# Identity multiplications at the boundaries between stages, taken out of a four-layer kernel on one core

## The chip, the core and the metric

The kernel runs on one NeuronCore of a Trainium2 chip. The metric is the time of one execution on the device, in microseconds (us). A core has a matrix engine (TensorE, PE in the rows; its weight loads are PEld), VectorE (DVE), ScalarE (ACT), GpSimd (POOL) and SyncE (SP), which here issues the weights' DMAs. TensorE's clock has two levels, 1.2 and 2.4 GHz; the profile gives the granted clock as a share of the full one, 0.50 or 1.00, or a mean between them.

## The reference

Two blocks of two layers each work on 256 rows of 1024 features, float32:

```python
for i in range(2):                                   # layers 0 and 1
    q, k, v = project_qkv(x, w_qkv[i], cos, sin)
    a = moba_attention(q, k, v) if i == 0 else sliding_window_attention(q, k, v, sinks)
    x = layer_norm(alpha * x + a @ w_o[i], ln_mix_g[i], ln_mix_b[i])
    f = swiglu(x, ...) if i == 0 else moe_swiglu(x, w_router, ...)   # 8 experts, top 2
    x = layer_norm(alpha * x + f, ln_ffn_g[i], ln_ffn_b[i])
    x = x + (p[i] @ w_ple_proj[i]) * sigmoid(x @ w_ple_gate[i])
for l in range(2):                                   # layers 2 and 3
    h = hybrid_mixer(rmsnorm(x, pre_mix_norm[l]), ...)   # delta rule and dilated attention
    x = x + rmsnorm(h, post_mix_norm[l])
    h = conv_glu_ffn(rmsnorm(x, pre_ffn_norm[l]), ...)
    x = x + rmsnorm(h, post_ffn_norm[l])
```

None of it contains the multiplications that this case is about.

## The kernel before

One core holds X, the 256 rows, as two row tiles of 128 rows (t = 0, 1). Every large product is made of three matmuls: an operand is split into a high and a low part (w_hi and w_lo for weights, xT_hi and xT_lo or aT_hi and aT_lo for activations), and mm3 (line 770) issues high x high, high x low and low x high. Weights stream in as units of 128 x 2048 values through six raw buffers; ScalarE casts the high part (line 520), VectorE subtracts the low part (line 525).

Each engine runs one program written out by hand, in order, with semaphore waits between engines. For this case TensorE's order at a boundary between two stages matters. A stage that starts from X needs X transposed. At a boundary X is being normalised, row tile after row tile, by VectorE and ScalarE. TensorE then does, in this order:

- turn_tile for t = 0: it waits until X of that tile is ready, and transposes it by 8 matmuls (line 750) in layers 0 and 1, or multiplies it by a diagonal matrix of the row scales, by 16 records of fp32 matmuls (line 748), in layers 2 and 3;
- keep_warm(n, b): it waits until bank b is free, and issues n matmuls of an identity by 512 columns of constants into that bank; nobody reads them, and the next turn writes over them;
- turn_tile for t = 1;
- tile_ready: it waits until the turned tiles are copied out and split (ScalarE's cast of xT_hi, line 1345; VectorE's xT_lo, lines 1793 and 1796, in layers 2 and 3 after line 1955, which applies the norm's weights);
- the next stage: the dense feed-forward in layer 0 (features, by mm3), the router and the experts in layer 1, the delta-rule mixer on entry into layers 2 and 3, and the feed-forward of layers 2 and 3.

```python
            def keep_warm(n, b):

                if M.free[b].n:
                    pe.wait_ge(M.free[b].sem, M.free[b].n)
                for _ in range(n):
                    nc.tensor.matmul(bank[b][:, :], ident, cst[:, 0:512], start=True, stop=True)
```

It is called with WARM_START once before the first stage (line 1282), with WARM_LN between attention and feed-forward of layers 0 and 1 (line 1286), and through enter (lines 1313 to 1323) with WARM_RMS on entry into layer 3 and before the feed-forward of layers 2 and 3; on entry into layer 2 the count is 0. The three constants stand in line 40.

Of the kernel before, what the change touches and what calls it, by code (L numbers as in the profile page):

```python
# [36 lines left out]
FF2 = 2816  # L37
NE = 8
UNIT = 2048
WARM_START, WARM_LN, WARM_RMS = 6, 5, 4  # L40
RAW = 6
SPLIT = 3
NEG = -1.0e30
# [2541 lines left out]
```

How the kernel before makes its waits and increments, by code:

```python
        def wait_loaded(E, eng, i):  # L485
            slot, n = i % RAW, 16 * (i // RAW + 1)
            if E.ev.turn is not None:
                n = n + E.ev.turn * (16 * TURN // RAW)
            eng.wait_ge(E.loaded[slot].sem, n)
            return raw[:, slot, :]
# [5 lines left out]
        def unit(E, pe, key, base=None):  # L496
            i = index(key, base)
            pe.wait_ge(*E.lo.at("unit", key_of(i)))
            return w_hi[:, place(i), :], w_lo[:, place(i), :]
# [11 lines left out]
        def split_hi(E, ac, i):  # L512
            src = wait_loaded(E, ac, i)
            back = i - SPLIT - (1 if any(i - SPLIT <= w < i for w in whole) else 0)
            if E is V and i < SPLIT:
                ac.wait_ge(E.groups.sem, 1 + E.ev.turn * plan.per.get("ovf_groups", 0))
            elif back >= 0:
                ac.wait_ge(*reader(E, back))
            nc.scalar.copy(w_hi[:, place(i), :], src).then_inc(*E.hi.mark("unit", i))
# [1 line left out]
        def split_lo(E, ve, i):  # L522
            ve.wait_ge(*E.hi.at("unit", i))
            nc.vector.tensor_tensor(w_lo[:, place(i), :], raw[:, i % RAW, :], w_hi[:, place(i), :].bitcast(F32), ALU.subtract) \
                .then_inc(*E.lo.mark("unit", i))
# [26 lines left out]
            def overflow_loads():  # L553
                sp.wait_ge(*flag_done.at())
                r = sp.value_load(flag_i[0:1, 0:1], min_val=0, max_val=1)
                with sp.If(r > 0):
                    sp.wait_ge(*M.put.at("last"))
# [83 lines left out]
            def load_both():  # L641
                gp.wait_ge(*params.last())
                for L in (2, 3):
```

## Time and profile before

| | |
|---|---|
| time before, median of 3 executions | 2372.84 us (2371.3 to 2373.51) |
| the profiled execution | 2372.58 us, of which 2370.8 us is the span from the first to the last instruction |
| TensorE busy in the span | 2233.2 us (94%) |
| VectorE, ScalarE, GpSimd busy | 1717.1, 1371.4, 54.3 us |
| mean granted TensorE clock | 0.969 |
| DMA | 573.37 MB, mean 242 GB/s |

How to read it: an engine's busy time is the time in which one of its instructions runs; matmuls overlap one another, so that the busy time of TensorE is the union of them. A matmul at half clock counts as just as busy as one at full clock, but takes longer: a busy share says nothing of speed, and the granted clock has to be read beside it. Where TensorE idles, the timeline names what it waited for.

### The profile page before, as it was taken

To read this page: it belongs to the slowest core of one execution; us is meant where nothing else is said; L and a number is where in the kernel's file an instruction comes from. 1 tells how busy PE (TensorE), PEld (TensorE's weight loads), DVE (VectorE), ACT (ScalarE), POOL (GpSimd) and SP (SyncE) were. 2 spreads that over 40 slices of the span, in tenths; PEclk is the share of its full clock that TensorE was granted. 3 is DMA by queue.
4 is the path that set the end of the run, shared out by engine and by line. 5 is a ranking of instruction groups with operands and counts; after the bars stand their busy time and mean duration, and the time that the engine had idled before them with its cause. 6 is when DMAs were issued, how large, how long until landed. Compare 5 with 4: busy or idle time off the path is not lost. (4 is left out here: it accounts for less than half of the span.)

```text
span 2370.8 us, 32516 instructions
## 1 busy us (share of the span) xinstructions
PE 2233.2 (94%) x12412; PEld 1907.0 (80%) x12412; DVE 1717.1 (72%) x1876; ACT 1371.4 (58%) x1423; POOL 54.3 (2%) x72
## 2 busy tenths in 40 slices
PE   7899999789999999999999999799899989889998
PEld 5689997568888888888888878598779978877997
DVE  5554546658888888888888898676657667665766
ACT  5433334537777777777777777462554446254444
POOL 2000000010000000000000020000000000000000
PEclk9799999989999999999999999899899999989999
DMA  9355554339999999999999999532325543132550
GB/s 391 141 200 180 193 180 176 108 107 378 378 378 372 384 373 378 377 381 373 377 376 380 372 385 371 190 125 72 125 107 179 195 160 110 72 116 103 182 195 37
DMA packets 81800, 573.37 MB, mean 242 GB/s; under 512 B 9552, under 2 KB 9664, under 8 KB 15984
## 3 DMA queue, kind: packets, MB, share of 16 engines
q1 hardware_dynamic: 76320, 545.82, 60.8%
q0 software_dynamic: 5376, 26.12, 3.0%
q8 instruction: 71, 1.16, 0.2%
q14 instruction: 33, 0.27, 0.0%
HBM read 564.03 MB, written 17.83 MB: 245 GB/s over the span
## 5 line engine op out<-in xcount | busy, mean ns | idle before, releaser
L525 DVE TENSOR_TENSOR w_lo<-raw,w_hi 128x2048 fp32r<-128x2048 f32 x508 | 1163.3, 2300 | 352.1 <-ACT w_hi L520 350.2
L520 ACT CAST w_hi<-raw 128x2048 fp32r<-128x2048 f32 x508 | 969.2, 1911 | 519.2 <-PE bank L770 513.9
L770 PE MATMUL bank<-w_hi,xT_hi 128*128 128x512 f32 x1184 | 468.2, 395 | 10.7 <-DVE w_lo L525 5.9
L770 PE MATMUL bank<-w_hi,xT_lo 128*128 128x512 f32 x1184 | 461.4, 390 | 0.0
L770 PE MATMUL bank<-w_lo,xT_hi 128*128 128x512 f32 x1184 | 460.9, 389 | 0.0
L770 PE MATMUL bank<-xT_hi,w_hi 128*128 128x256 f32 x1344 | 383.6, 285 | 6.9 <-DVE xT_lo L1796 5.0
L770 PE MATMUL bank<-xT_hi,w_lo 128*128 128x256 f32 x1344 | 383.0, 285 | 0.0
L770 PE MATMUL bank<-xT_lo,w_hi 128*128 128x256 f32 x1344 | 382.9, 285 | 0.0
L770 PE MATMUL bank<-w_hi,aT_hi 128*128 128x512 f32 x864 | 346.4, 401 | 15.3 <-DVE aT_lo L2007 9.5
L770 PE MATMUL bank<-w_hi,aT_lo 128*128 128x512 f32 x864 | 338.8, 392 | 0.0
L770 PE MATMUL bank<-w_lo,aT_hi 128*128 128x512 f32 x864 | 338.8, 392 | 0.0
L770 PEld LDWEIGHTS bank<-w_hi,xT_hi 128*128 128x128 f32 x1184 | 222.3, 188 | 63.9 <-DVE w_lo L525 11.6
L770 PEld LDWEIGHTS bank<-xT_hi,w_hi 128*128 128x128 f32 x1344 | 260.8, 194 | 8.8 <-DVE xT_lo L1796 5.3
L770 PEld LDWEIGHTS bank<-xT_lo,w_hi 128*128 128x128 f32 x1344 | 260.6, 194 | 1.2
L770 PEld LDWEIGHTS bank<-xT_hi,w_lo 128*128 128x128 f32 x1344 | 260.4, 194 | 0.0
L770 PEld LDWEIGHTS bank<-w_hi,xT_lo 128*128 128x128 f32 x1184 | 222.2, 188 | 47.1
L770 PEld LDWEIGHTS bank<-w_lo,xT_hi 128*128 128x128 f32 x1184 | 222.4, 188 | 45.0 <-issue 0.7
L770 PEld LDWEIGHTS bank<-w_hi,aT_hi 128*128 128x128 f32 x864 | 164.2, 190 | 50.3 <-issue 18.4
L770 PEld LDWEIGHTS bank<-w_hi,aT_lo 128*128 128x128 f32 x864 | 163.5, 189 | 35.5
L770 PEld LDWEIGHTS bank<-w_lo,aT_hi 128*128 128x128 f32 x864 | 164.2, 190 | 30.9
L1479 ACT ACTIVATE arena<-bank,fcw 128x256 f32<-128x256 f32 x88 | 44.9, 560 | 61.3 <-PE bank L770 61.3
L1615 ACT COPY arena<-bank 128x512 f32<-128x512 f32 x24 | 14.1, 586 | 91.9 <-PE bank L1164 91.9
(318 smaller groups left out, 1700.8 us busy)
## 6 DMA issues: line engine op xcount, KB each, us to landing
raw<-in_wu_eg SPq DMA_DIRECT2D x112, 1024.0 KB, 7.2
raw<-in_wu_eu SPq DMA_DIRECT2D x112, 1024.0 KB, 7.2
raw<-in_wu_ed SPq DMA_DIRECT2D x112, 1024.0 KB, 7.1
raw<-in_wu_up SPq DMA_DIRECT2D x44, 1024.0 KB, 4.8
raw<-in_wu_ffn_gu SPq DMA_DIRECT2D x28, 1024.0 KB, 4.8
raw<-in_wu_in SPq DMA_DIRECT2D x28, 1024.0 KB, 4.8
raw<-in_wu_down SPq DMA_DIRECT2D x22, 1024.0 KB, 4.8
raw<-in_wu_ffn_d SPq DMA_DIRECT2D x14, 1024.0 KB, 4.8
```

Source lines behind the costliest of these rows:

```text
L520: nc.scalar.copy(w_hi[:, place(i), :], src).then_inc(*E.hi.mark("unit", i))
L525: nc.vector.tensor_tensor(w_lo[:, place(i), :], raw[:, i % RAW, :], w_hi[:, place(i), :].bitcast(F32), ALU.subtract) \
L770: mm = nc.tensor.matmul(o, l[i], r[j], start=(first and n == 0), stop=(last and n == 2), skip_group_check=not lone)
L1479: ins = nc.scalar.activation(buf[:, s % 2, m, :], bank[b + half][:, m * S:(m + 1) * S], ACT.Identity, bias=fcw[:, c, 3:4], scale=fcw[:, c, ...
L1615: nc.scalar.copy(dn["Xl"][:, t * DN_H:(t + 1) * DN_H, :], bank[t][:, :].rearrange("p (h n) -> p h n", n=P)) \
```

## The change

Two constants are set to zero. The loops in keep_warm then issue nothing at the boundaries; the wait before them and all else stays, and the six multiplications at the start stay too.

```diff
-WARM_START, WARM_LN, WARM_RMS = 6, 5, 4
+WARM_START, WARM_LN, WARM_RMS = 6, 0, 0
```

## Rows read from the trace of the kernel before

**Rows 1.** The page, TensorE's granted clock in 40 equal slices, in tenths.

```profile
PEclk9799999989999999999999999899899999989999
```

**Rows 2.** Windows of two feed-forward stages: length, busy PE PEld DVE ACT POOL, clock, DMA.

```profile
127.50:356.00 228.50, 228.50 (x1634) 216.95 (x1635) 115.72 (x80) 83.96 (x54) 0.00 (x0) 0.99 0.53 187
...
2176.00:2349.00 173.00, 173.00 (x1248) 164.28 (x1247) 121.18 (x144) 84.58 (x84) 0.00 (x0) 1.00 0.44 155
```

**Rows 3.** The line of the identity multiplications: ns min/median/max, first and last start.

```profile
L765 PE MATMUL bank<-cst x56: 592/592/1220, 9.6 to 2164.5; 128*128 128x512 f32 x56
...
  issue: 12.2, 44
```

**Rows 4.** Timeline, layer 0, attention to feed-forward: start us, us, instruction, [idle before <-releaser].

```profile
118.02 1.03 PE L750 MATMUL bank<-cst,X 128*128 128x128 f32 x8
...
118.89 4.46 PE L765 MATMUL bank<-cst 128*128 128x512 f32 x10
...
123.09 1.28 DVE L1921 SCALAR_TENSOR_TENSOR X<-R,small,vec 128x1024 f32<-128x1024 f32 x1
...
124.43 1.09 PE L750 MATMUL bank<-cst,X 128*128 128x128 f32 x8 [1.08 <-DVE X L1921]
...
127.42 0.35 PE L770 MATMUL bank<-xT_hi,w_hi 128*128 128x256 f32 x1 [1.90 <-DVE xT_lo L1793]
```

**Rows 5.** Timeline, layer 1, attention to router.

```profile
507.96 1.28 DVE L1921 SCALAR_TENSOR_TENSOR X<-R,small,vec 128x1024 f32<-128x1024 f32 x1
...
509.31 0.14 PEld L750 LDWEIGHTS bank<-cst,X 128*128 128x128 f32 x1 [0.25 <-DVE X L1921]
...
509.72 1.04 PE L750 MATMUL bank<-cst,X 128*128 128x128 f32 x8
```

**Rows 6.** Timeline, layer 2, mixer to feed-forward; layer 3 repeats it from 2161.49 on.

```profile
1745.96 3.60 PE L765 MATMUL bank<-cst 128*128 128x512 f32 x8
...
1750.87 2.05 PE L748 MATMUL bank<-R,X 128*128 128x128 f32 x16 [1.31 <-DVE R L1946]
...
1752.13 1.52 DVE L1955 TENSOR_TENSOR arena<-bank,prew 128x512 f32<-128x512 f32 x2
...
1755.41 0.35 PE L770 MATMUL bank<-xT_hi,w_hi 128*128 128x256 f32 x1 [2.50 <-DVE xT_lo L1796]
```

**Rows 7.** Timeline, entry into layer 3.

```profile
1957.65 2.05 PE L748 MATMUL bank<-R,X 128*128 128x128 f32 x16
...
1959.49 1.29 DVE L1796 TENSOR_TENSOR xT_lo<-arena,xT_hi 128x512 fp32r<-128x512 f32 x2 [1.89 <-ACT xT_hi L1345]
...
1963.80 0.28 PE L1096 MATMUL bank<-xT_hi,wba_hi_lo 128*16 128x256 f32 x1 [4.09 <-DVE xT_lo L1796]
```

**Rows 8.** Windows behind the five boundaries, and one at full clock (131.23).

```profile
127.82:131.23 3.41, 3.41 (x18) 3.41 (x17) 3.41 (x2) 0.00 (x0) 0.00 (x0) 0.50 0.59 177
131.23:134.64 3.41, 3.41 (x31) 3.41 (x30) 0.27 (x1) 0.00 (x0) 0.00 (x0) 1.00 1.01 423
513.53:516.94 3.41, 3.41 (x18) 2.06 (x16) 3.41 (x2) 1.64 (x1) 0.00 (x0) 0.50 0.44 119
520.35:527.18 6.83, 5.53 (x26) 5.43 (x27) 4.79 (x27) 2.63 (x4) 1.64 (x2) 0.50 0.35 143
1755.98:1759.39 3.41, 3.41 (x19) 3.41 (x18) 3.41 (x2) 0.12 (x1) 0.00 (x0) 0.50 0.29 65
...
1964.19:1967.60 3.41, 3.41 (x19) 2.49 (x17) 1.45 (x1) 0.36 (x1) 0.00 (x0) 0.50 0.28 46
2172.40:2175.82 3.42, 3.42 (x19) 3.42 (x18) 2.63 (x2) 0.00 (x0) 0.00 (x0) 0.50 0.50 170
```

**Rows 9.** Turns with no multiplications before them: timeline rows, and the window around the second.

```profile
1505.46 1.97 PE L750 MATMUL bank<-cst,X 128*128 128x128 f32 x8 [4.87 <-DVE X L1921]
...
1539.13 6.31 PE L748 MATMUL bank<-R,X 128*128 128x128 f32 x32 [4.09 <-DVE R L1946]
...
1537.52:1544.35 6.83, 5.22 (x24) 5.22 (x25) 2.88 (x7) 5.57 (x10) 0.00 (x0) 0.50 0.00 0
```

## The prediction

> **What bounds the kernel now.** I read the page first, for the share of TensorE and for its clock; then the windows of the long dense stages, to learn whether time lost by TensorE comes back anywhere; then the line of the removed instructions; then the timeline around each place where they stand; and last the windows at either clock level, to price the clock. The page's clock row shows a kernel that is mostly at full clock, 9 tenths, with dips to 8 and 7 [rows 1]: the clock falls somewhere in many slices. The windows of the feed-forward stages of layers 0 and 3 have TensorE busy for the whole of 228.5 us and 173.0 us [rows 2]. There is no idle time in them in which a late start could be made good. So whatever TensorE loses at the door of such a stage reaches the end of the program in full, and whatever it does while it would otherwise stand idle costs nothing.
>
> The multiplications in question are the second kind of thing on their face. They are the 28 fp32 matmuls of line 765, each of which the trace holds as two records, 56 in all [rows 3]; nobody waits for them. 6 stand at the start and stay; 5 stand at each of two boundaries and 4 at each of three, 22 in all, and go. In layer 0 the ten records of five matmuls run for 4.46 us from 118.89, and end at 123.35. The turn of the second row tile (8 transposes, line 750) needs X, which VectorE writes from 123.09 to 124.37, and starts at 124.43 [rows 4]. TensorE has 1.08 us to spare after its last idle multiplication: these do not delay the turn.
>
> **The change part by part.**
>
> Removed instructions on TensorE's queue. In four of the five places nothing is won. Layer 0: 1.08 us to spare, as said [rows 4]. Boundary to the feed-forward of layer 2: the turn starts at 1750.87, right when the diagonal of line 1946 is there [rows 6], and the four matmuls, which take 3.60 us, were issued 4.9 us earlier; that of layer 3 repeats it. Entry of layer 3: the turn's first matmul starts at 1957.65 [rows 7], 0.05 us after the last filler has streamed; I take 0. Boundary of layer 1 is the exception: X is ready at 507.96 + 1.28 = 509.24, the turn's first weights load at 509.31, and yet its matmuls come at 509.72 [rows 5], because the fifth filler is still streaming. Here the removal wins about 0.35 us. The wait for the bank that stands before the fillers stays in the program, and is one that the turn has to pass anyway: 0.
>
> The clock, term A, the turns. What the fillers change is what TensorE did before the clock is granted. Layer 0 without them: TensorE is dense until about 119.05 (1.03 us from 118.02), then idle until 124.43, 5.4 us instead of 1.1, then busy for 1.09 us, then idle until 127.42 [rows 4]. The trace has two boundaries of just this shape and without fillers. Entering layer 2, after 4.09 us of idling, the 32 records of both turns took 6.31 us, 0.197 us each, in a stretch at 0.50 [rows 9]; 16 of them at full clock take 2.05 us, 0.128 each [rows 6]. And the turn at 1505.46, after 4.87 us of idling, took 1.97 us for 8 transposes [rows 9] against 1.09 [rows 4]. So I expect the second turn of a boundary at 1.2 GHz. It lies on the path: at layer 0 the chain goes turn, cast on ScalarE, subtraction on VectorE, first multiplication. Layer 0: 1.97 - 1.09 = +0.9 us. Layer 1: only 3.8 us pass between the first turn and the second, so the clock may fall in the middle of it: between 0 and +0.9, I take +0.5. Layers 2 and 3, feed-forward: 16 x 0.197 = 3.15 against 2.05, +1.1 us each, all of it on the path, as VectorE takes the turned halves one after the other at 1752.13 [rows 6]. Entry of layer 3: VectorE is not done with the first tile before 1959.49 + 1.29 = 1960.78 [rows 7], when a turn at half clock that began at 1957.65 is through at 1960.8: 0, at most 0.2. A = 0.9 + 0.5 + 1.1 + 0 + 1.1 = 3.6 us (bounds 0 and 4.2).
>
> Term B, the dense stage behind the turn. Today, too, every one of the five boundaries has a fall: just after the stage has begun there is one stretch of 3.4 us at 0.50 with 18 or 19 matmuls in it, where the next 3.4 us at 1.00 hold 31 [rows 8]. The fillers do not prevent the fall in this execution; they put it off until the stage runs. One such stretch costs 12 of 31 matmuls, 12 x 0.11 = 1.4 us. Without fillers the clock is low already when the stage begins, and has to be earned back by dense work: the half-clock part of the stage may be somewhat shorter than 3.4 us, or up to nearly 6.8, the length of the two low stretches that had idle time at their head [rows 8, 9]. The extra is so between 0 and +1.4 us for each; I take the middle, 0.7, for layers 0, 2 and 3 (feed-forward). In layer 1 the stage behind is the router's 24 short matmuls, half of which run low already: +0.35. Entry of layer 3: a full idle gap of 4.09 us stands between the turn and the stage whatever the fillers do [rows 7]: 0. B = 3 x 0.7 + 0.35 = 2.45 us (bounds 0 and 5).
>
> Term C, executions other than the profiled one. That all five falls happen is a matter of how the idle gap of 1.9 to 2.5 us lies to the moments at which the clock is set. Other executions may be spared some that the longer gap never is. The profiled execution took 2372.58 us and the median of the three others is 2372.84, so it was not an unlucky one by much. I take 0.8 of a fall, 0.8 x 1.4 = 1.1 us, with bounds 0 and 3 falls, 4.2 us.
>
> Sum: -0.35 + 3.6 + 2.45 + 1.1 = +6.8 us on the profiled execution's 2372.58 (of which 2370.8 is the span), 2379.4; the median stands 0.26 above it, so 2379.6 us, 0.29% slower.
>
> A rule against term A: the transposes of line 750 took 1.97 us in a stretch at 0.50 [rows 9] and 1.09 at 1.00 [rows 4], so here they follow the granted clock. The Trainium skill, "TensorE: Matmul & The Clock Gate", Part 4: PE-mode transpose, says that full clock doesn't engage for transposes, which do not count as busy work in the same way. By it the turns of layers 0 and 1 would lose nothing, 1.4 us less in the sum; the trace disagrees on their speed, and no row separates whether they count as work.
>
> **The rivals.**
>
> 1. Slower by the clock, as summed. For it: the falls after 4 and 5 us of idling [rows 9], and TensorE without a gap behind [rows 2].
>
> 2. Only a shift. The clock falls earlier and so is back earlier: each boundary keeps one low stretch, part of it under idle time. Then B is 0 or negative, C is 0, and half of A stays hidden by the work of ScalarE and VectorE: 1.8 - 0.35 = +1.5 us, 2374.3 us, no measurable change. For it: every boundary has its fall today [rows 8]. Against it: the low stretches with idle time at their head are twice as long.
>
> 3. Not slower: the fillers' place in TensorE's queue. They hold the turn of layer 1 back by 0.35 us [rows 5], and the one of layer 3's entry by at most 0.1 [rows 7]. If the clock took no notice of them (a multiplication by an identity might not count as work), only this is left: 2372.84 - 0.45 = 2372.4 us. It decides if the second turns still run at 1.00 after the change. Against it: layer 2's entry without fillers ran its turns at 0.50, layer 3's with them at 1.00 [rows 7, 9].
>
> 4. Worse: the low clock feeds itself, since a slower turn makes the gap longer for the next. The whole 6.8 us at half clock at four boundaries, instead of 3.4: 4 x 1.4 = 5.6, with A's 4.2 and C's 4.2, +14, 2386.8 us.
>
> 5. Fewer than named. The change speaks of six boundaries; the diff sets two constants, and the sixth, the entry of layer 2, has a count of 0 already. That costs nothing in the sum, which counts 22 instructions.
>
> **How the numbers follow.** Rival 1: 0.70. Rival 2: 0.14. Rival 3: 0.06. Rival 4: 0.10. The likeliest gives 2379.6 us. About 4.7 us (0.2%) is what a measurement of this kernel can tell from no change. The likeliest case itself runs from +2.5 to +13 (A, B and C near their bounds), so part of it, about 0.10, falls within 0.2%. The range reaches down to 2374.0, into the shift, and up to 2387.5, over most of case 4. Slower by over 0.2%: 0.60 + 0.10 + a little of case 2, hence 0.72. Within 0.2%: 0.25. Faster: 0.03, since the rows allow a gain of no more than half a microsecond, and only something that they do not show could give more.
>
> **What would show it.** In the profile of the changed kernel: line 765 with 12 records, all at the start. The second turn of layer 0 at about 2.0 us instead of 1.09, and those before the feed-forward of layers 2 and 3 at about 3.1 instead of 2.05, in windows at 0.50 (term A). The low stretch at each of these doors beginning before the turn and reaching 3.4 to 6.8 us into the stage, the same stages still without a gap (term B). Layer 1's turn 0.4 us sooner after X. Entry of layer 3 unchanged in length. The prediction is wrong if the turns keep 1.00; or if the clock is back before the stage begins, which is the shift; or if the stages behind show idle time that takes the loss in.

## Result, and the profile after

| | before | after |
|---|---|---|
| median of 16 executions | 2372.53 us | 2375.79 us |
| ratio to before, with its 95% interval | | 1.0017 (1.0009 to 1.0025) |
| profiled execution's span | 2370.8 us | 2373.6 us |
| mean granted clock | 0.969 | 0.963 |
| TensorE busy | 2233.2 us | 2218.8 us |

The change makes the kernel slower, by 0.17% or 4 us (2 to 6), where +6.8 us was forecast. The ratio is not that of the two medians: these lie 3.3 us apart, the means of the same executions 4.0. (One execution of a kernel further down, the half-filled one, took 4459 us and is left out of its ratio.) TensorE does 44 records fewer, is busy for 14.4 us less, and the program ends later. The page's clock row shows little of it: against [rows 1], slices 8 and 30 (counted from 1) have 8 tenths where they had 9, and slice 2 has 8 where it had 7. Slice 30 holds the door of layer 2's feed-forward; slices 2 and 8 hold none of the edited places.

```profile
PEclk9899999889999999999999999899889999989999
```

Line 765 is left with the 12 records at the start:

```profile
L765 PE MATMUL bank<-cst x12: 592/592/1222, 9.6 to 16.0; 128*128 128x512 f32 x12
```

At the door of layer 0's feed-forward (timeline of after, start us, us, instruction, idle before it; to be read beside [rows 4]):

```profile
120.57 1.28 DVE L1921 SCALAR_TENSOR_TENSOR X<-R,small,vec 128x1024 f32<-128x1024 f32 x1
...
121.95 1.94 PE L750 MATMUL bank<-cst,X 128*128 128x128 f32 x8 [5.41 <-issue]
...
125.63 0.55 PE L770 MATMUL bank<-xT_hi,w_hi 128*128 128x256 f32 x1 [1.74 <-issue]
```

The reader sees the idle gap of 5.41 us, the turn at 1.94 us instead of 1.09, and the stage's first multiplication at 0.55 us instead of 0.35: the turn and the stage's beginning are both at half clock. From X to the stage it is 5.06 us, and was 4.33: +0.73 us. (The trace as a whole stands 2.5 us earlier at this point, ahead of the first edit: the first stage began 1.2 us earlier, and a low stretch in the attention of layer 0 is shorter. That is why places are compared by their own lengths here.)

At the door of layer 1's router, against [rows 5], first the router's first multiplication in before, then after:

```profile
512.75 0.28 PE L770 MATMUL bank<-xT_hi,wr_hi 128*8 128x256 f32 x1 [1.99 <-DVE wr_lo L2377]
```

```profile
509.45 1.29 DVE L1921 SCALAR_TENSOR_TENSOR X<-R,small,vec 128x1024 f32<-128x1024 f32 x1
...
510.84 1.70 PE L750 MATMUL bank<-cst,X 128*128 128x128 f32 x8 [3.77 <-issue]
514.34 0.37 PE L770 MATMUL bank<-xT_hi,wr_hi 128*8 128x256 f32 x1 [1.80 <-DVE wr_lo L2377]
```

The turn comes 1.39 us after X is begun instead of 1.76: 0.37 us won, as no filler is in the way. Its 1.70 us instead of 1.04 take that back: from X's begin to the router it is 4.89 us, and was 4.79.

At the door of layer 2's feed-forward, against [rows 6]; layer 3's repeats it (turn 3.75 us, and 6.25 us from turn to stage):

```profile
1751.89 3.75 PE L748 MATMUL bank<-R,X 128*128 128x128 f32 x16 [4.80 <-issue]
1754.05 0.69 DVE L1955 TENSOR_TENSOR arena<-bank,prew 128x512 f32<-128x512 f32 x1 [0.87 <-PE bank L748]
...
1755.69 0.69 DVE L1955 TENSOR_TENSOR arena<-bank,prew 128x512 f32<-128x512 f32 x1 [0.94 <-PE bank L748]
...
1758.14 0.55 PE L770 MATMUL bank<-xT_hi,w_hi 128*128 128x256 f32 x1 [2.49 <-DVE xT_lo L1796]
```

VectorE now waits for each half of the turn (0.87 and 0.94 us). From turn to stage it is 6.25 us, and was 4.54: +1.71 us.

At the entry of layer 3, against [rows 7]:

```profile
1961.45 3.46 PE L748 MATMUL bank<-R,X 128*128 128x128 f32 x16 [3.45 <-issue]
1963.24 1.29 DVE L1796 TENSOR_TENSOR xT_lo<-arena,xT_hi 128x512 fp32r<-128x512 f32 x2 [1.89 <-PE bank L748]
...
1967.55 0.28 PE L1096 MATMUL bank<-xT_hi,wba_hi_lo 128*16 128x256 f32 x1 [2.63 <-DVE xT_lo L1796]
```

The turn is slow as well, 3.46 us, and it costs nothing: turn to stage 6.10 us, and was 6.15.

How much of each stage runs at half clock. Windows of after, cut at the stage's first multiplication: length, busy PE PEld DVE ACT POOL, clock, DMA (against [rows 8]):

```profile
118.57:125.63 7.06, 1.94 (x9) 1.60 (x9) 6.04 (x10) 3.26 (x4) 1.59 (x3) 0.50 0.70 245
125.63:128.81 3.18, 3.18 (x15) 3.18 (x16) 3.18 (x2) 0.00 (x0) 0.00 (x0) 0.50 0.38 108
1750.15:1758.14 7.99, 3.75 (x16) 3.52 (x17) 5.48 (x11) 4.47 (x8) 0.00 (x0) 0.50 0.00 0
1758.14:1763.80 5.66, 5.66 (x26) 5.66 (x27) 4.09 (x2) 0.70 (x1) 0.00 (x0) 0.50 0.48 178
...
2173.70:2176.80 3.10, 3.10 (x14) 3.10 (x15) 3.10 (x2) 0.69 (x1) 0.00 (x0) 0.50 0.10 21
```

Before, each stage had 3.4 us of it. Now the clock is low for 7 to 8 us ahead of the stage, and then for 3.18, 5.66 and 3.10 us in it. The low subtraction that VectorE makes some 10 us into the stage tells what that costs. Layer 2, the same instruction in before and in after, two fences:

```profile
1764.91 2.29 DVE L525 TENSOR_TENSOR w_lo<-raw,w_hi 128x2048 fp32r<-128x2048 f32 x1 [5.41 <-ACT w_hi L520]
```

```profile
1768.63 2.29 DVE L525 TENSOR_TENSOR w_lo<-raw,w_hi 128x2048 fp32r<-128x2048 f32 x1 [6.40 <-ACT w_hi L520]
```

It is 3.72 us later, and the stage began 2.73 us later: 0.99 us in the stage. In layers 0 and 3 the same step gives -0.08 and -0.11 us.

So the five boundaries of this pair of profiles cost: layer 0 0.73 - 0.08 = 0.65; layer 1 0.1; layer 2 1.71 + 0.99 = 2.7; entry of layer 3 0; layer 3 1.67 - 0.11 = 1.6. Together 5.0 us. The spans differ by 2.8: -2.5 us of that arose ahead of the first edit, so that the program behind it is 5.3 us longer. The rest of the program, which has no edit in it, went otherwise in the two executions, up and down:

```profile
2101.00:2152.50 51.50, 42.69 (x216) 32.67 (x215) 23.09 (x67) 25.81 (x63) 1.05 (x2) 0.83 0.23 82
352.20:500.90 148.70, 127.45 (x648) 97.56 (x647) 94.14 (x219) 69.78 (x144) 1.58 (x3) 0.95 0.35 126
```

```profile
2104.50:2153.50 49.00, 40.45 (x216) 30.98 (x215) 22.99 (x67) 25.81 (x63) 1.05 (x2) 0.86 0.25 86
350.30:502.40 152.10, 131.41 (x648) 100.71 (x647) 94.41 (x219) 69.81 (x144) 1.58 (x3) 0.92 0.34 123
```

The first fence is before, the second after; each row covers the same instructions (216 and 648 matmul records in both). The attention of layer 3 is 2.5 us shorter at a clock of 0.86 instead of 0.83, the stretch from the end of layer 0's feed-forward to layer 1's attention 3.4 us longer at 0.92 instead of 0.95. Against such swings only many executions of each kernel carry a verdict.

### The profile page after: what moved, and what is told of

The parts are those of the page before. It is cut to its first block and busy times, and to the rows that moved or that the text cites. A ratio compares the mean times of both kernels' runs of the same rounds, so it can differ in the third digit from the quotient of the medians.

```text
span 2373.6 us, 32428 instructions
## 1 busy us (share of the span) xinstructions
PE 2218.8 (93%) x12368; PEld 1904.4 (80%) x12368; DVE 1718.2 (72%) x1876; ACT 1372.0 (58%) x1423; POOL 58.0 (2%) x72
```

## Experiments

The fillers are the identity multiplications of keep_warm and whatever stands in their place. The theory: they are worth what they do to TensorE's clock, and nothing else. The rivals: they only hold up TensorE's queue (a gain if they go); or the low stretch is merely shifted. Medians are in us, ratios to the kernel before on the same chip, with 95% intervals.

### Which boundaries

```diff
-WARM_START, WARM_LN, WARM_RMS = 6, 5, 4
+WARM_START, WARM_LN, WARM_RMS = 6, 0, 4
```

> Only the fillers of layers 0 and 1 are taken out (counts 6, 0, 4). Theory (slow clock at the door of the stage): in the pair of profiles the boundary of layer 0 cost +0.65 us and that of layer 1 +0.1 us, and an execution that is spared falls today loses more, so +0.5 to +2.5 us, middle +1. The second turn of layer 0 takes about 1.95 us instead of 1.09. Rival (the fillers only hold up TensorE's queue): -0.35 us, turn at 1.09.

Measured: 2374.57, ratio 1.0009 (1.0001 to 1.0018). Its second turn in layer 0, and the window around it:

```profile
121.58 1.94 PE L750 MATMUL bank<-cst,X 128*128 128x128 f32 x8 [5.42 <-issue]
...
120.30:130.50 10.20, 7.19 (x32) 6.84 (x33) 8.16 (x7) 1.63 (x3) 1.55 (x3) 0.50 0.60 212
```

The clock is at half for 10.2 us, 5.2 of them behind the stage's start at 125.26, where the changed kernel had 3.18: here the stage's part was the large one.

```diff
-WARM_START, WARM_LN, WARM_RMS = 6, 5, 4
+WARM_START, WARM_LN, WARM_RMS = 6, 5, 0
```

> Only the fillers of layers 2 and 3 are taken out (counts 6, 5, 0). Theory: in the pair of profiles +2.75 and +1.6 us at the two feed-forward doors and 0 at the entry of layer 3, so +2.5 to +4.5 us, and together with the run that takes out those of layers 0 and 1 the two make up the whole change's +4. The two turns take about 3.75 us instead of 2.05. Rival (only a shift of the low stretch): +1.5 us or less.

Measured: 2374.30, ratio 1.0015 (1.0006 to 1.0024). The turn of layer 2 took 3.75 us and the stage began 6.34 us after it, against 3.75 and 6.25 us in the changed kernel. Both halves of the change cost time, as expected, the first barely clear of its interval. Their sum, +5.7 us by the ratios (+5.4 by the medians), and the whole change's +4 lie within each other's intervals; the +3.6 of layers 2 and 3 (+2.6 by the medians) is within what was expected of them, and the queue's -0.35 is excluded for layers 0 and 1.

### Filling the gap behind the second turn

```diff
                 turn_tile((L, "mix"), 1, lambda t: x_ready.at(L, "mix", t))
+                keep_warm(2, turn_bank((L, "mix"), 0, 0))
...
                         turn_tile((L, which), t, lambda t: prenorm.at(L, which, t), True)
+                    keep_warm(2 if which == "mix" else 4 if L == 3 else 0, turn_bank((L, which), 0, 0))
```

> All fillers of before stay, and further ones are added behind the second turn of the same five boundaries (2, 2, 2, 2, and 4 at the entry of layer 3), into the bank that the first tile has left, to fill the idle gap of 1.9 to 4.1 us before the stage. Theory: the falls that before has behind each boundary (18 matmuls in 3.4 us instead of 31) vanish; each is worth 1.4 us, so up to -7 us, -4 to -6 in the mean as some executions are spared some already. If the clock doesn't see such multiplications as work, or if the fillers hold up the stage: 0 to +2 us.

Measured: 2364.53, ratio 0.9969 (0.9957 to 0.9981), 7.4 us faster than before. The windows behind the boundaries in its trace:

```profile
125.13:128.54 3.41, 3.40 (x28) 3.41 (x29) 3.41 (x2) 0.00 (x0) 0.00 (x0) 1.00 0.63 198
1752.90:1756.30 3.40, 2.85 (x24) 2.88 (x25) 3.40 (x3) 1.21 (x1) 0.00 (x0) 1.00 0.00 0
1961.10:1964.50 3.40, 3.39 (x29) 3.02 (x30) 1.84 (x1) 0.36 (x1) 0.00 (x0) 1.00 0.17 36
510.60:514.00 3.40, 2.95 (x25) 2.00 (x25) 2.74 (x2) 2.87 (x4) 0.00 (x0) 1.00 0.30 110
2168.90:2172.00 3.10, 3.10 (x28) 3.10 (x27) 0.75 (x1) 0.33 (x1) 0.00 (x0) 1.00 0.90 365
```

All of them are at 1.00, with 28 or 29 matmuls (fewer where the window begins ahead of the stage or the router has ended) where [rows 8] has 18 or 19: the five falls are gone. By the start times of the same matmuls in this trace and in that of before, that makes the heads of the five stages 6.2 us shorter (about 1.5 us each, the router 0.2). What is won at the entry of layer 3 is lost again, as the clock falls once more in its stage, 25 us on, at 1989.4; and 2.5 us of the whole come from the attention of layer 3, which has no edit. This is the theory's strongest test. More work without a reader was added (24 records) and the kernel became faster. It beats both kernels of the case, and the gain is a little more than the 4 to 7 us that were expected.

With the same additions, but the fillers ahead of the second turn taken out:

```diff
-WARM_START, WARM_LN, WARM_RMS = 6, 5, 4
+WARM_START, WARM_LN, WARM_RMS = 6, 0, 0
```

> The fillers before the second turn are out, as in the change, and the ones behind it are in (2, 2, 2, 2, 4). Theory: the 5.4 us gap ahead of the second turn lets the clock fall before the turn (term A stays, 3 to 4 us), but the low stretch is paid off by fillers instead of the stage's own matmuls, so that the stage's part (term B) mostly goes: between 0 and +3 us against before, 1 to 4 us faster than the change. If only the total of fillers mattered, not their place, it would equal before.

Measured: 2369.18, ratio 0.9992 (0.9984 to 1.0001). The door of layer 2:

```profile
1751.44 3.75 PE L748 MATMUL bank<-R,X 128*128 128x128 f32 x16 [4.79 <-issue]
1754.99 2.71 PE L765 MATMUL bank<-cst 128*128 128x512 f32 x4
1757.69 0.36 PE L770 MATMUL bank<-xT_hi,w_hi 128*128 128x256 f32 x1
```

The turn is at half clock, 3.75 us; four filler records take 2.71 us instead of 1.88, being partly at half clock themselves; and the stage begins at full clock, 0.36 us for its first matmul. Term A is there, and the low part of the stage is gone, today's as well as what term B added. By the medians the kernel is 6.6 us faster than the changed one (5.9 by the ratios), which is more than the 1 to 4 us expected, and 4.7 us slower than the one with both gaps filled (5.5 by the ratios); from before it can't be told apart. So filling the gap behind the turn is worth about 6 us where the one ahead is open and about 7 where it is filled (2371.7 to 2364.5), and filling the gap ahead 4 to 5 us, each give or take 2 us.

```diff
                 def enter(which, warm):
+                    if L == 2 and which == "in":
+                        keep_warm(4, turn_bank((L, which), 0, 0))
...
+                    keep_warm(2 if which == "mix" else 4 if L == 3 else 2, turn_bank((L, which), 0, 0))
```

> The kernel with both gaps filled, plus the sixth boundary, the entry of layer 2, that has no fillers in before: 4 ahead of its first turn and 2 behind its second. Theory: the 32 records of the turns there fall from 6.31 us to about 4 and the low stretch behind them goes: 1.5 to 4 us faster than the kernel with both gaps filled, 2360 to 2363 us. If the fall there comes from the embedding gate's own tail and not from the gap: no change, 2364.5.

This is the kernel with both gaps filled, and the entry of layer 2 besides. Measured: 2364.11, ratio 0.9964 (0.9953 to 0.9976). The turns of the sixth boundary, in the kernel with both gaps filled and in this one (two fences):

```profile
1537.31 6.20 PE L748 MATMUL bank<-R,X 128*128 128x128 f32 x32 [4.09 <-DVE R L1948]
...
1546.37 0.37 PE L1096 MATMUL bank<-xT_hi,wba_hi_lo 128*16 128x256 f32 x1 [2.86 <-DVE wba_hi_lo L2462]
```

```profile
1536.15 3.84 PE L748 MATMUL bank<-R,X 128*128 128x128 f32 x32 [0.65 <-DVE R L1950]
...
1543.95 0.28 PE L1096 MATMUL bank<-xT_hi,wba_hi_lo 128*16 128x256 f32 x1 [2.25 <-DVE wba_hi_lo L2464]
```

The turns fell to 3.84 us as expected, but the stage begins only 1.3 us sooner after them (7.80 us for 9.06), as 2.25 us of idle time are left behind the fillers, and the clock still falls in it. In the medians 0.4 us is to be seen, less than the intervals can tell; the expected gain of 1.5 us and more did not come.

### How much filling, and of what kind

```diff
-WARM_START, WARM_LN, WARM_RMS = 6, 5, 4
+WARM_START, WARM_LN, WARM_RMS = 6, 3, 2
```

> Counts 6, 3, 2 instead of 6, 5, 4: the fillers cover half of the first gap, 2.6 of 5.4 us in layers 0 and 1 and 1.7 of 4.9 in layers 2 and 3. If the clock needs only some work in the gap: equal to before, 2371.5. If any long idle stretch makes it fall: layers 2 and 3 cost most of what taking all out does, layer 0 and 1 little: +1 to +3.5 us.

Measured: 2375.84, ratio 1.0017 (1.0008 to 1.0026): half of the filling is worth no more than none in the whole time, give or take 2 us. Its profile says something else of the boundaries. The second turns of layer 1 (1.09 us), of layer 2 and of layer 3's entry (2.05 us each) kept full clock, and those of layer 0 (1.96 us) and of layer 3's feed-forward did not. From a door's turn to its stage it is 0.7 us longer than before in layer 0 and 1.7 in layer 3, and unchanged in the other three, where the changed kernel lost 2.2 us more. What made the profiled execution as long as the changed kernel's is a place without an edit: the stretch between layer 0's feed-forward and layer 1's attention, 3.4 us longer than before here as there. The rows are layer 2's turn, then layer 3's fillers, which end at 2166.99, and turn. The gap of 3.04 us is the same, and only in layer 3 is the turn at half clock:

```profile
1754.50 2.05 PE L748 MATMUL bank<-R,X 128*128 128x128 f32 x16 [3.04 <-DVE R L1946]
...
2165.11 1.88 PE L765 MATMUL bank<-cst 128*128 128x512 f32 x4
2170.03 3.78 PE L748 MATMUL bank<-R,X 128*128 128x128 f32 x16 [3.04 <-DVE R L1946]
```

Transposes in the place of the multiplications:

```diff
-                    nc.tensor.matmul(bank[b][:, :], ident, cst[:, 0:512], start=True, stop=True)
+                    for c in range(8):
+                        nc.tensor.transpose(bank[b][:, (c % 4) * P:(c % 4 + 1) * P], cst[:, (c % 4) * P:(c % 4 + 1) * P], ident)
```

> Each filler of before becomes 8 transposes of 128 by 128 constants, about as long (8 x 0.109 = 0.87 us against 0.86). If transposes count as work for the clock: equal to before within 1 us, second turn of layer 0 at 1.09 us, clock 1.00 through it. If they don't, as the Trainium skill, "TensorE: Matmul & The Clock Gate", Part 4, has it: equal to the change or worse, as those at the start of the program stop counting too, +4 to +8 us, second turn at 1.95.

Measured: 2371.06, ratio 0.9995 (0.9986 to 1.0004), equal to before. In layer 0 its filler of 4.31 us is followed by a turn of 1.09 us, and the clock is 1.00 throughout:

```profile
116.78 4.31 PE L766 MATMUL bank<-cst 128*128 128x128 f32 x38
...
122.10 1.09 PE L750 MATMUL bank<-cst,X 128*128 128x128 f32 x8 [1.01 <-DVE X L1922]
...
118.00:125.70 7.70, 4.80 (x42) 4.35 (x41) 7.29 (x11) 3.16 (x4) 1.59 (x3) 1.00 0.70 246
```

Transposes held the clock as multiplications did. The rule that the prediction weighed against term A, in the Trainium skill, "TensorE: Matmul & The Clock Gate", Part 4, is not borne out here, for fp32 transposes: the measurement decides.

One row of the array instead of 128:

```diff
-                    nc.tensor.matmul(bank[b][:, :], ident, cst[:, 0:512], start=True, stop=True)
+                    nc.tensor.matmul(bank[b][:, :], ident[0:1, :], cst[0:1, 0:512], start=True, stop=True)
```

> Every filler of before stays in its place and count, but multiplies one row of the identity by one row of constants (1 partition instead of 128), so that it keeps TensorE just as long with 1/128 of the array. Theory that the clock goes by time with columns streaming: equal to before within 1 us, second turn of layer 0 at 1.09 us. Theory that it goes by how much of the array works: equal to the change, +4 us, second turn at 1.95 us.

Measured: 2386.63, ratio 1.0058 (1.0044 to 1.0071), slower than either expectation. Here the fillers at the start failed too: the 12 records took 10.60 us,

```profile
8.79 10.60 PE L765 MATMUL bank<-cst 1*128 1x512 f32 x12 [8.79 <-DMA cst<-in_cst]
```

and the first stage started at half clock: its matmuls take 0.63 us up to 22.5, and 0.39 from then on. To part the two, the start was made whole again:

```diff
+                    if n == WARM_START:
+                        nc.tensor.matmul(bank[b][:, :], ident, cst[:, 0:512], start=True, stop=True)
+                    else:
+                        nc.tensor.matmul(bank[b][:, :], ident[0:1, :], cst[0:1, 0:512], start=True, stop=True)
```

> As the one-row kernel, but the 6 multiplications at the start of the program are whole again; only the 22 at the boundaries use one row of the identity and of the constants. Theory: the clock goes by how much of the array works, so that the one-row fillers don't hold it, run at half clock themselves and then hold the turns up as well. The 3.4 us lost at the start come back, and the rest stays: 2378 to 2384 us, more than taking the fillers out (2375.8). Rival: all of the 14 us came from the start and from chance: 2372 to 2376.

Measured: 2376.99, ratio 1.0024 (1.0015 to 1.0033), a little under the range expected and a little over the rival's; from the changed kernel's 1.0017 and 1.0020 it can't be told apart. So 8 to 10 us of the one-row kernel's 14 hang on the start. 2.45 us of these are the fillers' own (10.60 us instead of 8.15 in before); the rest is open. Layer 0's door:

```profile
116.17 6.75 PE L768 MATMUL bank<-cst 1*128 1x512 f32 x10
...
120.28 1.29 DVE L1924 SCALAR_TENSOR_TENSOR X<-R,small,vec 128x1024 f32<-128x1024 f32 x1
...
122.86 1.97 PE L750 MATMUL bank<-cst,X 128*128 128x128 f32 x8
```

TensorE is busy all through, and yet the ten records take 6.75 us instead of 4.46: the clock fell under them. They end at 122.9, after X (121.57), so that they hold the turn up by 1.2 us, and then it runs at half clock besides. Busy time alone did not hold the clock. Whether the number of rows decides, or the values in them (one row of the identity holds a single 1, all of it 128), was not separated.

### The change again

> The changed kernel once more, for a second execution with its boundaries laid out otherwise to the clock. Theory: the second turns at half clock again (1.7 to 2.0 and 3.4 to 3.8 us), 3.7 and 6.25 us from the start of the turn to the stage in layers 0 and 2; the low part of each stage between 3 and 6 us, so that the five boundaries sum to +4 to +7 us against the profile of before; the median near 2375.8. If the stage's part is on average as long as today's: +4.

Measured: 2375.89, ratio 1.0020 (1.0011 to 1.0029). The turns were at 1.94, 1.68, 3.75, 3.46 and 3.76 us, and the span of its profile was 2372.2 us: the boundaries cost the same, and the program up to the last feed-forward ran the same within 0.5 us; the end of the program came out 1.4 us shorter than in the first profile.

## Why the prediction was right in sign and too high

Three of its terms were off: A 1.0 us too low, B 1.65 and C about 1 us too high. The time fell inside the range, helped by errors that run both ways and by a range 13.5 us wide.

**What bounds the kernel.** Right. The dense stages have no gap, and what was lost at their doors was not made up in them.

**The removed instructions.** Right: 0.37 us won in layer 1 (0.35 was forecast), nothing elsewhere.

**Term A.** Right in its mechanism, a little low in its size: 3.6 was forecast. By place: layer 0 +0.73 (0.9), layer 1 +0.1 with the gain taken in, that is about +0.45 (0.5), layers 2 and 3 +1.71 and +1.67 (1.1 each), entry of layer 3 0 (0). The sum is 4.6. What was mis-sized is the turn in layers 2 and 3: 16 records at 0.197 us each were read off a turn [rows 9] that ran partly at full clock at its end (it ends at 1545.44, and the low stretch at 1544.35). All at half clock they take 3.75 us, not 3.15.

**Term B.** The step that failed. Forecast was +2.45 us, each stage's low part half as long again. In the pair of profiles it was -0.08, +0.99 and -0.11 us in the three feed-forwards and about 0 in layer 1, so +0.8 us. The stretch that began 7 to 8 us ahead of the stage ended some 3 us into it in layers 0 and 3, as today's does, and 5.7 us into it in layer 2; the second profile of the changed kernel has the same (3.3, 5.7 and 3.2 us). Taking the middle of the bounds at every door was the fault: the extra came at one of three. It is no fixed rule of a place, as the run without the fillers of layers 0 and 1 had 5.2 us of it in layer 0's stage. That the slow turn is itself work by which the clock is earned back is a reading, not shown. The price of a fall was about right: 12 x 0.11 is 1.3 and not 1.4, and filling the second gap gave back 1.5 us at a door.

**Term C.** Forecast was +1.1 us for falls that other executions of before are spared. The traces of before and of the runs that leave a boundary as it was (the two halves and the transposes) show the feed-forward doors of layers 0, 2 and 3 with their fall each time, as in [rows 8], so the spared falls are few. The times leave room for some: three of the 16 executions of before took 2367.1, 2367.9 and 2369.5 us, and none of the changed kernel less than 2374.9. They make the difference of the means 0.7 us larger than that of the medians; none of the three was profiled, so that it isn't known whether they were spared falls at these doors. C is so at most 0.7 us in the means, and near 0 in the medians.

With A at 4.6, the gain of 0.37, B at 0.8 and C at 0, the boundaries give +5.0, and two measurements +4.0 and +4.7 by the ratios (1.0017 and 1.0020), +3.3 and +4.2 by the medians. The rest, about -1 us, is in the parts without an edit, where the low stretches fall otherwise. In both profiles of the changed kernel the attention of layer 3 was 2.5 us shorter and the stretch from layer 0's feed-forward to layer 1's attention 3.4 us longer. The first of these goes with the edit of layers 2 and 3 in the traces kept: the run without those fillers has it too (49.0 us at a clock of 0.86), and the run without the fillers of layers 0 and 1, the transposes and the half filling don't (51.5 us at 0.83 in each). But it stands in the kernel with both gaps filled as well. Why is open, and so is the second, which the half filling shares. No experiment was made on either.

**Rivals.** Only a shift (+1.5 us) had its truth in term B and not in A; the time lies about midway between its sum and the likeliest one. The queue (-0.45) fell with both halves of the change. The low clock that feeds itself did not come about, nor did the forecast's upper half. The time lies in the range, and by the bound of 0.2% it falls just within no change, which had 0.25; slower by over 0.2%, which had 0.72, did not come. The bound was set too wide for this measurement: its interval was 0.08% to either side, and excludes no change.

## What to carry to other kernels

An instruction with no reader can be worth its place if it keeps TensorE's clock up across a gap that ends on the critical path; before it is cut, look at the granted clock behind the gap and not at the busy share. And where fillers already stand, look for the gap that they leave: here filling the one behind the turn, 1.9 to 4.1 us long, was worth 6 to 7 us, more than the fillers in place with their 4. When a slow stretch is priced, price what stands in it at half clock in full, and do not add as a matter of course that it reaches further into the next stage: here it did so at one door of three.

## What was not expected of the hardware

- TensorE busy without a pause is not enough for full clock: ten records of one row by 512, back to back, did not keep the clock from falling to 1.2 GHz in mid-stream and took 6.75 us, where with 128 rows they held 2.4 GHz and took 4.46, and transposes of 128 by 128 held it too.
- Half of a gap filled held the clock at three turns of five, and with the same gap of 3.04 us left it held in layer 2 and not in layer 3. The whole time shows nothing of that (1.0017 against 1.0017 and 1.0020).
- At half clock a turn of 16 records takes 3.75 us against 2.05, and one of 8 transposes 1.97 against 1.09: these short records stretch by 1.8, and so hold up the engines behind them.
